# Reordering an attention round: values' products between the two heads' transposes, output copied ahead of the scores

## What is computed

```python
s = einsum('qd,kd->qk', q, k) * 64 ** -0.5      # + bias or mask in the first block
p = softmax(s, axis=-1)
o = einsum('qk,kd->qd', p, v)
```

## Time and profile before

| | us |
|---|---|
| median of 3 runs | 3041.06 (3039.77 to 3041.84) |
| the profiled execution | 3041.17 |
| its span in the trace | 3038.6 |
| TensorE busy | 2692.9 (89%) |
| VectorE busy | 1535.9 (51%) |
| GpSimd busy | 1294.6 (43%) |
| ScalarE busy | 1026.3 (34%) |

### The profile page before, as it was taken

The page is one execution under the profiler, slowest core; times in us unless marked ns, Lnnn a source line. Parts: engine busy times, 40 slices in busy tenths (PEclk is TensorE's granted clock), DMA queues, the critical chain, the costliest instruction groups (busy, mean ns, idle before and its releaser), DMA issues. The chain is left out here.

```text
span 3038.6 us, 37066 instructions
## 1 busy us (share of the span) xinstructions
PE 2692.9 (89%) x14304; PEld 2183.0 (72%) x14304; DVE 1535.9 (51%) x2279; ACT 1026.3 (34%) x1739; POOL 1294.6 (43%) x654
## 2 busy tenths in 40 slices
PE   1799669989999788888789999998799999699998
PEld 1587447868888565665578888886787888578886
DVE  2423424655445524555675555555577686632223
ACT  2333323232222433333431221113455555432222
POOL 2335554444444445555623333333344444344443
PEclk9899879999999899999999999998899999799999
DMA  5423222433334200000023333331111111022221
GB/s 193 150 93 114 98 79 101 148 125 130 132 133 138 69 29 15 25 18 15 35 98 124 119 125 112 118 111 53 49 42 63 43 56 49 35 83 97 97 97 70
DMA packets 78526, 264.53 MB, mean 87 GB/s; under 512 B 8464, under 2 KB 12688, under 8 KB 78352
## 3 DMA queue, kind: packets, MB, share of 16 engines
q1 hardware_dynamic: 70416, 248.67, 23.4%
q10 hardware_dynamic: 7648, 12.19, 1.3%
q0 software_dynamic: 288, 1.31, 0.1%
HBM read 258.99 MB, written 3.15 MB: 86 GB/s over the span
## 5 line engine op out<-in xcount | busy, mean ns | idle before, releaser
L1916 POOL TENSOR_TENSOR SLO<-RAW,SHI 128x1024 fp32r<-128x1024 f32 (+1 forms) x336 | 816.0, 2430 | 1215.7 <-ACT SHI L1754 1215.6
L1754 ACT ACTIVATE SHI<-RAW 128x1024 fp32r<-128x1024 f32 (+1 forms) x336 | 346.5, 1034 | 1199.9 <-PE PS L2175 1166.1
L2173 PE MATMUL PS<-HLh,SHI 128*128 128x512 f32 x1680 | 686.6, 409 | 24.3 <-DVE HLl L1985 15.2
L2174 PE MATMUL PS<-HLl,SHI 128*128 128x512 f32 x1680 | 659.6, 393 | 0.0
L2175 PE MATMUL PS<-HLh,SLO 128*128 128x512 f32 x1680 | 659.2, 392 | 0.0
L2173 PEld LDWEIGHTS PS<-HLh,SHI 128*128 128x128 f32 x1680 | 318.6, 190 | 118.4 <-issue 41.7
L2173 PE MATMUL PS<-hh,SHI 128*128 128x512 f32 (+1 forms) x944 | 352.8, 374 | 19.3 <-DVE hl L2065 9.9
L2175 PEld LDWEIGHTS PS<-HLh,SLO 128*128 128x128 f32 x1680 | 317.9, 189 | 69.1
L2174 PEld LDWEIGHTS PS<-HLl,SHI 128*128 128x128 f32 x1680 | 319.2, 190 | 65.2 <-issue 7.5
L2174 PE MATMUL PS<-hl,SHI 128*128 128x512 f32 (+1 forms) x944 | 347.0, 368 | 0.0
L2175 PE MATMUL PS<-hh,SLO 128*128 128x512 f32 (+1 forms) x944 | 346.9, 367 | 0.0
(11 more groups left out here) (227 smaller groups left out, 3957.0 us busy)
## 6 DMA issues: line engine op xcount, KB each, us to landing
RAW<-in_k_w SPq DMA_DIRECT2D x316, 512.0 KB, 3.2
ADA<-in_k_w SPq DMA_DIRECT2D x132, 512.0 KB, 4.1
early<-in_k_w SPq DMA_DIRECT2D x12, 512.0 KB, 10.7
RAW<-in_k_w SPq DMA_DIRECT2D x20, 256.0 KB, 2.7
XL<-in_xT ACTq DMA_DIRECT2D x1, 2048.0 KB, 12.4
bi<-in_k_bias ACTq DMA_DIRECT2D x16, 128.0 KB, 2.2
out<-XL SPq DMA_DIRECT2D x8, 256.0 KB, 2.1
bi<-in_k_bias ACTq DMA_DIRECT2D x8, 192.0 KB, 3.2
```

The lines of the kernel that those rows point to most:

```text
L1754: eng.activation(u.hi, u.w, ACT.Copy).then_inc(S["a_hi"], 1)
L1916: eng.tensor_tensor(u.lo, u.w, u.hi.bitcast(F32), ALU.subtract).then_inc(S["g_lo"], 1)
L2173: eng.matmul(st.out, lh, rh, start=st.first and j == 0, stop=False)
L2174: eng.matmul(st.out, lh, rl, start=False, stop=False)
```

## The change

The order within a round, the noted work of a transpose, one engine, one buffer and one weight:

- a round now does s2 of the first head of pair i-2; yield; s3 of pair i-3; yield; s2 of the second head; yield; finish of pair i-3; shares of pair i-1; s1 of pair i; yield
- the first head of a pair is divided on ScalarE, the second on GpSimd as before
- the transposes count for half the work in `weave`; attention's weight in the second block goes from 1.1 to 1.25 (in the first it stays at 0.6)
- three `pt` buffers in place of two

```diff
-Share = namedtuple("Share", "e m t_exp t_rec t_done")
+Share = namedtuple("Share", "on e m t_exp t_rec t_done")
...
-                work[0] += 128 * 4 * (j1 - j0)
+                work[0] += 128 * 2 * (j1 - j0)
...
-        def shares(it):
-
-            e, m, t_exp = st[id(it)]
-            t_rec, t = tick("v_rec"), tick("g_share")
-            put(Share(e.ap[:, 0:it["n"]], m.ap, t_exp, t_rec, t))
-            m.free = [t]
-            st[id(it)] = (e, t)
+        def shares(pair):
+
+            for on, it in zip("ag", pair):
+                e, m, t_exp = st[id(it)]
+                t_rec, t = tick("v_rec"), tick(on + "_share")
+                put(Share(on, e.ap[:, 0:it["n"]], m.ap, t_exp, t_rec, t))
+                m.free = [t]
+                st[id(it)] = (e, t)
...
         for i in range(n + 4):
+            turn, read = 0 <= i - 2 < n, 0 <= i - 3 < n
+            if turn:
+                s2(pairs[i - 2][0])
+                yield
+            if read:
+                done = s3(pairs[i - 3])
+                yield
+            if turn:
+                s2(pairs[i - 2][1])
+                yield
+            if read:
+                finish(pairs[i - 3][0], *done)
+                if "done" in pairs[i - 3][1]:
+                    emitted.add(pairs[i - 3][1]["done"])
             if 0 <= i - 1 < n:
-                for it in pairs[i - 1]:
-                    shares(it)
-            if 0 <= i - 3 < n:
-                out_of[i - 3] = s3(pairs[i - 3])
-                yield
-            if 0 <= i - 2 < n:
-                for it in pairs[i - 2]:
-                    s2(it)
-                yield
+                shares(pairs[i - 1])
             if i < n:
                 for key in pairs[i][0].get("needs", ()):
                     yield from after(key)
...
                 yield
-            if 0 <= i - 3 < n:
-                finish(pairs[i - 3][0], *out_of.pop(i - 3))
-                if "done" in pairs[i - 3][1]:
-                    emitted.add(pairs[i - 3][1]["done"])
...
-               "pt": (2, 768, F32, 4), "f": (4, 512, F32, 4), "r": (2, 512, F32, 4),
+               "pt": (3, 768, F32, 4), "f": (4, 512, F32, 4), "r": (2, 512, F32, 4),
...
-               "pt": (2, TT, F32, 4), "m": (8, 8, F32, 4)}, blk, c_at)
+               "pt": (3, TT, F32, 4), "m": (8, 8, F32, 4)}, blk, c_at)
...
-    weave((attention(heads, W, make2), 1.1), (pipelined(dense), 1.0))
+    weave((attention(heads, W, make2), 1.25), (pipelined(dense), 1.0))
...
+            def share(st):
+                if st.on == "a":
+                    a.wait_ge(st.t_rec)
+                    eng.activation(st.e, st.e, ACT.Copy, scale=st.m[:, 3:4]).then_inc(S["a_share"], 1)
...
             def share(st):
-                g.wait_ge(st.t_rec)
-                eng.tensor_scalar(st.e, st.e, st.m[:, 3:4], None, ALU.mult).then_inc(S["g_share"], 1)
+                if st.on == "g":
+                    g.wait_ge(st.t_rec)
+                    eng.tensor_scalar(st.e, st.e, st.m[:, 3:4], None, ALU.mult).then_inc(S["g_share"], 1)
```

More of the change, by code:

```diff
@@ L706, in attention @@
     def attention(items, W, finish):
-        st, out_of = {}, {}
+        st = {}
         def s1(pair):
@@ L1895, in _ @@
             own = {Dma: dma_, Table: table, Silu: silu_c, Split: split, Square: square_, Rstd: rstd_, NormA: norm_a,
-                   VCopy: vcopy, HSq: hsq, HNorm: hnorm, Score: score, Flip: flip_, OutSplit: osplit, Gate: gate,
+                   VCopy: vcopy, HSq: hsq, HNorm: hnorm, Score: score, Share: share, Flip: flip_, OutSplit: osplit, Gate: gate,
                    GSum: gsum, SiluF: silu, Up: up, LowerB: lowerb, Sigm: sigm, GateF: gate_f, GateX: gate_x,
```

## The result

The changed kernel takes 3059.9 us (median of 4 runs, 3057.6 to 3068.7), the kernel before 3040.5 us: a ratio of 1.0069, 95% interval 1.0048 to 1.0089. That is 0.7% slower and past the upper end of my range (3023 to 3058), where I had forecast 3044, no change that can be measured. The profiled execution took 3068.7 us, 9 us above its median. A second measurement of the same kernel gave 3060.1 against 3043.2 us, ratio 1.0055 (1.0039 to 1.0072), and its profiled execution, at 3060.0 us, is the typical one. I use both and say which.

What follows compares the result with a forecast made beforehand. TensorE, 89% busy, bounds the kernel, with room only in the two attention places. Second block -38.0 - 3.6 + 43.2 + 3 = +4.6, first block -2: +3 on 3041.2 gives 3044 us, range 3023 to 3058.

Steps and rivals of the forecast that it cites:

- The order by hand: Walk through `weave` with the noted work, before and after: in the second block attention waits for dense from head tile 4.
- the list of signs: Second block: no low-part waits, scores waiting about 3 us for L1931 before three head tiles, TensorE idle near 56 us.
- neighbourhood rounds 0: First block's neighbourhood rounds: no change, at worst +2 us from a division behind a 2.4 us weight split on GpSimd.
- The clock I leave as it is: Second block: no clock term, since old and new order have about one cluster of waits per head tile.
- The gain: Second block: 38.0 us of TensorE's waits for the output's low part and transpose copies go, and 3.6 of small waits.
- The division on ScalarE: Second block: late division shows 0.6 to 1.35 us in eight context rounds, 7.0 us; latent scores and a tile hide it.
- (b): Second block: attention catches up with dense, adding query-tile chains, slow-clock stretches and shown divisions; 3057 us in the middle, chance 0.22.
- the chains of head tiles 4 to 7: Second block: attention waits for query tiles' norm, rotation and scores; 4.7 us for tile 4, 13.8 for tiles 5 to 7.
- the two terms for tiles in the rounds: Second block: bank waits in 14 rounds with output tiles, 10.5 us, and where three query tiles end in latent rounds, 7.2.
- my removed 38.0: Second block's attention: transposes' and projections' waits for the output's low part and earlier transposes' copies, all 38.0 us taken as gone.
- (a): Second block: cover works better than counted because waits don't add up; 3017 us at the most, 3030 with half, chance 0.30.
- (c): Whole kernel: the change does less than it says, banks order the work and both sums shrink together; 3041 us, chance 0.10.

Runs made afterwards that it cites:

- the best kernel: Changed kernel with old noted work and weight in `weave` and both divisions on GpSimd at the start of the round: 2996.0 us, ratio 0.9850.

## Why the prediction was wrong, step by step

**What was read rightly.** The order by hand held: no wait for the low part before the last scores of the second block, waits of scores for the rotation at head tiles 4 to 7 (four, 11.2 us together; the sum has all four, the list of signs only three), of products for copies and additions. From the first scores to the end of attention ScalarE got 32.4 us more (I said 36), GpSimd lost 84.9 (85; the narrow divisions that moved are 16, not as many as the wide ones), and TensorE is idle 56.0 us (56). The modulation tiles: 29.7 us against 28.3. The dilated rounds come every 5.5 us, as said. The division of 128x768 takes 0.93 us against my 0.90.

**The step that failed** is the one with nothing in it: "neighbourhood rounds 0 (at worst +2, a division behind a 2.4 us weight split on GpSimd)". It cost 19 us (211.6 to 230.4 and 230.8). I had gone through the list to the end for the second block and not for the first. The same walk shows that with the halved noted work a value tile ends directly before the tail of a round at three places, and what ends with it (two splits, 2.0 us, and a modulation tile, 1.3 us) stands ahead of a division that the change puts directly before the scores. I had thought of a split on GpSimd and not of ScalarE, to which the change had just moved the division that comes first.

**"The clock I leave as it is"** was the second: four waits of 2.9 us became 10.2 us of idle time and 8.6 of busy time in the neighbourhood stretch. Not every microsecond is doubled like this: the second block's two profiles, with nearly the same idle time, stand at 0.93 and 0.96.

**The second block came out nearly right, by errors that cancel, which is luck.** I said +4.6, and up to the end of attention it was +4.4 and -1.8 us in the two profiles (+0.2 and -5.8 up to the last scores). Its terms, from the kernels that have them alone, all up to the last scores:
- The gain: -41.6, with all waits of the earlier trace rows gone. The early output split alone took 31.3 from this stretch (390.5 to 359.2); the 42 us by which that kernel is faster as a whole have parts elsewhere, 7 of them in the dilated attention. So the term was a third too large, and its inside is not right either: only the waits for the low part went, 22.4 us less idle; the waits for copies stayed (10.8 us of 13.3), and 8.9 of the 31.3 are busy time, the clock going from 0.96 to 0.98.
- The division on ScalarE: 7.0, for context rounds, "latent scores and a tile hide it". Measured 20.6 at the early place (352.8 to 373.4), and 9 with the products ahead of both heads' transposes. I looked at who waits for the division, and not at what stands behind it in ScalarE's queue; in the changed order this term was too small by 14 us. Rival (b) had it in latent rounds too, 16 in all with 0.3 us a round where it is up to 0.93.
- The numbers: 18.5 (the chains of head tiles 4 to 7) and the two terms for tiles in the rounds, 17.7, together 36.2. Measured 11 to 17 in the changed order (373.9 to 384.7 and 390.7) and 23 in the best one (352.8 to 375.5): too large by 13 to 25 us.
- The products between the heads and the third buffer were in my removed 38.0 and at 0. Measured for the whole kernel: nothing with ScalarE (3022.8 and 3022.7), and 3000.0 to 2996.0 with GpSimd, with intervals that overlap. In this stretch alone the products between the heads gave 7 us with GpSimd (359.8 to 352.8) and cost 4 with ScalarE (369.0 to 373.4).

**The rivals.** (a) fell: idle time is not under 45 us and the clock not near 1.00. (b) has 3059.9 inside its 3053 to 3061, with the four chains that it named, but it had put the loss in the second block, and it is in the neighbourhood stretch: its total is right by luck. (c), both sums shrinking together, fits the second block as far as the waits for the copies go, and not the total.

The whole change as a chain of kernels, each with one part more than the one before: early output split -42; third buffer 0; products between the heads -4 at most; one division on ScalarE +27; its late place +2; the new numbers +35, of them 20 where they meet the late place. That the parts add up to +18, with 17 and 19 measured, follows from their being steps of one chain; in another order they have other sizes, as the numbers show (+26 alone, +16 with early divisions, +30 in the best kernel). One edit of the change was worth more than I gave the whole of it, and two others, ScalarE for a division and the noted work, gave it back.

**The page's rule.** I had weighed a sentence of the Trainium skill (Perfetto Trace Analysis, Optimization Strategy), that a repeated gap can mean too little SBUF or PSUM for the next tile, as one that speaks for the gap only moving. The runs decide otherwise for this kernel: with the same four banks and the same two buffers the gap went away as soon as the bank was read earlier, and a third buffer added nothing. The other rule, on short idle times while going round the banks and a clock that falls and rises (TensorE: Matmul & The Clock Gate, A second HAM failure mode: psum-queue depth-cycling), gave rival (a) and holds here: the clock of the second block's attention rose from 0.96 to 0.98 with the waits for the low part gone, and is 1.00 in the best kernel. Where I was wrong was to let the wrong terms on the other side outweigh it.

**Left open.** What the 1.4 and 3.7 us behind attention are: over all kernels this stretch takes 1536.1 to 1543.2 us and goes with no single part. Why the second block's clock differs between two profiles of one kernel. And whether a form between the old and the new noted work beats 2996.0; the weight makes no difference that was measured.

## What to carry to other kernels

When an instruction moves, read the queue of its engine in both directions: what stands ahead of it when it is wanted (here two weight splits and, by way of the reciprocals, a modulation tile), and what it now stands ahead of (here the copy that the next products need). A division that waits for nothing and is wanted by nobody yet cost 27 us by being in a short queue in front of something urgent, while the slower engine, with 2.2 us in place of 0.93 but nothing urgent behind it, did it almost unseen; at a place directly before its reader the same comparison turns round, by 80 us.

A shortage of buffers that one early release removes is a matter of order: move the release first, alone, and measure, before adding buffers, engines and weights. And walk the whole list for every stretch to which a scheduling number applies, above all the one that seems to have nothing to do with it.

## What the runs showed of the hardware

Waits of 2.9 us between full stretches cost about as much again in the clock: in the neighbourhood stretch 892 records of the same products took 194.4 us busy at a granted clock of 0.93 and 201.6 at 0.89. Many short waits did not: in the second block's attention, twenty waits of at most 1.2 us are the main part of 17.3 us more idle time, and the busy time grew by 3.3 us only, at 1.00 and 0.99.

GpSimd's division of 128x384 takes 1.25 us and, where it starts while VectorE's modulation tile of 128x1024 (1.27 us) runs, 2.21 us, as in the row at 185.94 above and at two more places of that kernel. A division that is already running when the tile starts isn't made longer: at 180.1 us of the kernel before, one of 1.25 us has the tile start 1.0 us into it. It goes the other way too: at 190.65 us of the kernel of the row above, where GpSimd's subtraction of 128x1024 (2.4 us) had started 0.2 us earlier, the tile itself takes 3.29 us. The Trainium skill (GPSIMD Engine Reference, Specifications) says that GpSimd shares its SBUF interfaces with VectorE and meets its instructions with two SBUF inputs; the modulation tile has two (`ADA`, `c`), and the trace agrees, with 0.96 us more.
